# Where the weight split of the expert stages runs: ScalarE and VectorE in the place of GpSimd

## The reference

```
q = (ht @ w_q).reshape(T, 8, 2, 128)
s = einsum('thpd,hpkd->thpk', q, sub_keys)
top_s, top_i = top_k(s, 16)                     # per head and half: 16 of 128 keys
best_s, best_c = top_k(sums of the pairs, 16)   # 16 of 256 pairs -> 16 of 16384 experts
gates = softmax(best_s)
u = expert_u[expert_idx]; act = gelu(einsum('td,thkd->thk', x, u))
v = expert_v[expert_idx]; out = einsum('thk,thkd->td', gates * act, v)
```

## Time and profile before

| | |
|---|---|
| median of 3 runs | 4019.38 us (4003.71 to 4023.93) |
| profiled execution: span from the first to the last instruction | 3969.4 us |
| PE busy | 3562.3 us, 90% |
| DVE busy | 2298.1 us, 58% |
| POOL busy | 2306.4 us, 58% |
| ACT busy | 797.8 us, 20% |
| mean granted TensorE clock | 0.941 of 2.4 GHz |

### The profile page before, as it was taken

How to read it: one execution, slowest core, us unless ns; L and a number is a source line. 1 busy time by engine, 2 the same in 40 slices (tenths; PEclk the granted TensorE clock), 3 DMA queues, 4 the chain that set the end, 5 groups by cost and what they waited for, 6 DMA issues and landing times.

```text
span 3969.4 us, 47909 instructions
## 1 busy us (share of the span) xinstructions
PE 3562.3 (90%) x16820; PEld 2877.3 (72%) x16820; DVE 2298.1 (58%) x3373; ACT 797.8 (20%) x1199; POOL 2306.4 (58%) x1012
## 2 busy tenths in 40 slices
PE   8986997999988999989999998777777799999997
PEld 6554985787767787868768776666666688888885
DVE  2434443442177645452225998787777547887883
ACT  2223212111144311220121112222222111111110
POOL 5330003787745566648766886343434478888885
PEclk9997998999999999989999998888888899999998
DMA  3110001222211222212222343333333555555641
GB/s 129 48 38 1 1 1 43 80 95 90 96 64 66 66 74 78 70 58 96 85 90 101 127 135 116 113 117 112 129 120 114 193 200 200 183 179 189 214 138 69
DMA packets 146107, 408.58 MB, mean 103 GB/s; under 512 B 11192, under 2 KB 43960, under 8 KB 143680
## 3 DMA queue, kind: packets, MB, share of 16 engines
q1 hardware_dynamic: 73616, 266.37, 20.0%
q10 hardware_dynamic: 72368, 140.68, 10.1%
HBM read 337.80 MB, written 69.21 MB: 103 GB/s over the span
## 4 chain that ended last, share of the span: by engine, by line
PE 70%; DVE 19%; issue 7%; ACT 2%; DVEq 1%; ACTq 1%; DMA 0%; POOL 0%; POOLq 0%
PE bank L310 18%; PE bank L311 18%; PE bank L312 18%; DVE oneL L1665 2%; PE bank L333 1%; DVE oneH L1664 1%; ACT arena L851 1%; PE bank L805 1%; PE bank L807 1%; PE bank L503 1%; PE bank L517 1%; PE bank L745 1%; DVE arena L1640 1%; PE bank L507 1%; DVE arena L1566 1%
## 5 line engine op out<-in xcount | busy, mean ns | idle before, releaser
L1235 POOL TENSOR_TENSOR ring_hi<-ring,cst 128x1024 fp32r<-128x1024 f32 x504 | 1018.8, 2021 | 1591.0 <-PE bank L312 1576.0
L1237 POOL TENSOR_TENSOR ring_lo<-ring,ring_hi 128x1024 fp32r<-128x1024 f32 x504 | 1288.4, 2556 | 39.5
L310 PE MATMUL bank<-xs,ring_hi 128*128 128x512 f32 x2616 | 1076.2, 411 | 77.6 <-DVE xs L1256 50.8
L311 PE MATMUL bank<-xs,ring_hi 128*128 128x512 f32 x2616 | 1047.5, 400 | 0.0
L312 PE MATMUL bank<-xs,ring_lo 128*128 128x512 f32 x2616 | 1044.1, 399 | 0.0
L851 ACT ACTIVATE arena<-bank 128x512 f32<-128x512 f32 (+5 forms) x655 | 436.1, 684 | 1980.1 <-PE bank L312 1291.3
L310 PEld LDWEIGHTS bank<-xs,ring_hi 128*128 128x128 f32 x2616 | 511.3, 195 | 210.4 <-issue 66.0
L312 PEld LDWEIGHTS bank<-xs,ring_lo 128*128 128x128 f32 x2616 | 508.8, 194 | 112.4
L311 PEld LDWEIGHTS bank<-xs,ring_hi 128*128 128x128 f32 x2616 | 511.2, 195 | 102.8 <-issue 1.8
L310 PE MATMUL bank<-gw,ring_hi 128*128 128x512 f32 x1024 | 401.8, 392 | 0.8 <-ACT arena L851 0.7
L311 PE MATMUL bank<-gw,ring_hi 128*128 128x512 f32 x1024 | 398.8, 389 | 0.0
(11 more groups left out here) (255 smaller groups left out, 3725.5 us busy)
## 6 DMA issues: line engine op xcount, KB each, us to landing
ring<-weights SPq DMA_DIRECT2D x504, 512.0 KB, 3.3
hidden<-arena ACTq DMA_DIRECT2D x128, 256.0 KB, 2.2
gates<-arena ACTq DMA_DIRECT2D x16, 2048.0 KB, 7.6
arena<-hidden ACTq DMA_DIRECT2D x16, 2048.0 KB, 11.1
arena<-gates ACTq DMA_DIRECT2D x16, 2048.0 KB, 18.0
xres<-x_t ACTq DMA_DIRECT2D x4, 512.0 KB, 7.2
out_t<-arena SPq DMA_DIRECT2D x1, 2048.0 KB, 7.1
arena<-ret_decay ACTq DMA_DIRECT2D x1, 1024.0 KB, 5.6
```

Source lines behind the costliest of these rows:

```text
L310: pe.matmul(out_, wh, x[0], start=start, stop=False, skip_group_check=True)
L311: pe.matmul(out_, wh, x[1], start=False, stop=False, skip_group_check=True)
L1235: pool.tensor_tensor(ring_hi[:, r % 2, :], ring[:, r, :], one, ALU.mult).then_inc(split_hi, 1)
L1237: pool.tensor_tensor(ring_lo[:, r % 2, :], ring[:, r, :], ring_hi[:, r % 2, :].bitcast(F32), ALU.subtract).then_inc(w_split, 1)
```

## The change

From the gate stage on (block `B_S` = 295), POOL no longer splits. ACT makes the high part (`expert_hi`), DVE the low part (`expert_lo`), each for the block three ahead (`LEAD`) of the one whose product is just done. `ring_lo` is laid over `ring` (the split is in place), `ring_hi` has four buffers; so four blocks can stand split, and SP loads a slot again only when its block is used. In the value stage gated hidden, its parts and the sums are woven in block by block. POOL keeps the 295 blocks before, now limited by loads alone, and does blocks 295 to 297. PE's instructions and their order stay.

```
-        ring_hi = sb("ring_hi", [P, 2, D], F32R)
-        ring_lo = sb("ring_lo", [P, 2, D], F32R)
+        ring_lo = nc.alloc_sbuf_tensor_at("ring_lo", [P, RING, D], F32R, offset=nc.sbuf_base - RING * D * 4)
+        ring_hi = sb("ring_hi", [P, RING, D], F32R)
@@ SP
-                    sp.wait_ge(w_split, i * RING + (r + 1 - RING))
+                    sp.wait_ge(block_used, i * RING + (r + 1 - RING))
@@ PE
-                pe.wait_ge(w_split, it * per + (n + 1))
+                if n < B_S:
+                    pe.wait_ge(w_split, it * per + (n + 1))
+                else:
+                    pe.wait_ge(u_lo, it * per + (n - B_S + 1))
@@ ACT
+            def expert_hi(n, it=0, per=0):
+                r = n % RING
+                act.wait_ge(loaded[r], it * (4 * per) + 16 * (n // RING + 1))
+                A(ring_hi[:, r, :], ring[:, r, :], ACT.Copy).then_inc(u_hi, 1)
...
+            act.wait_ge(u_hi, LEAD)
             with act.Fori(0, NTG // 2) as i:
...
                         gelu(B_U + j0 + bb, q + bb, j0 + bb, i, 2 * NU_GATES)
+                        expert_hi(B_S + bb + LEAD, i, 2 * NU_GATES)
                         for u in (2 * b, 2 * b + 1):
...
+            def v_feed(g, it=0):
+                for b in range(JG):
+                    expert_hi(B_V + JG * g + b + LEAD, it, 2 * JG)
+                    gated_hi(g + 1, b, it)
+            v_feed(0)
             load(3)
             with act.Fori(0, NJG // 2 - 2) as i:
-                gated_hi(2, i)
+                v_feed(1, i)
                 load(4, i)
...
@@ POOL
-                if it is not None or r >= 2:
-                    pool.wait_ge(block_used, n - 1)
...
+            for n in range(B_S, B_S + LEAD):
+                split(n % RING, n - B_S, n // RING, u_hi, u_lo)
@@ DVE
+            def expert_lo(n, it=0, per=0):
+                r = n % RING
+                ve.wait_ge(u_hi, it * per + (n - B_S + 1))
+                TTN(ring_lo[:, r, :], ring[:, r, :], ring_hi[:, r, :].bitcast(F32), ALU.subtract).then_inc(u_lo, 1)
...
             with ve.Fori(0, NTG // 2) as i:
                 for u in range(2 * TG // 4):
+                    if u % 2 == 0:
+                        expert_lo(B_S + u // 2 + LEAD, i, 2 * NU_GATES)
                     ve.wait_ge(oh_pe, i * 16 + u + 1)
...
+            def v_feed(g, it=0):
+                for b in range(JG):
+                    expert_lo(B_V + JG * g + b + LEAD, it, 2 * JG)
+                    gated(g + 1, b, it)
+                    if b == 0 and g:
+                        acc(g - 1, 1, it)
+                    if b == 4:
+                        acc(g, 0, it)
+                    gated_lo(g + 1, b, it)
```

More of the change, by code:

```diff
@@ L68 @@
 N_LOADED = -(-N_BLOCKS // RING) * RING
+B_S = B_U + NU_ROUTE * TT
+LEAD = 3
 PARAMS = [("attn_pre", 8), ("attn_post", 8), ("mu", 15), ("w0", 4), ("a0", 4), ("k_k", 4), ("k_a", 4),
@@ L209, in build @@
         split_hi = sem("split_hi")
+        u_hi, u_lo = sem("expert_hi"), sem("expert_split")
         scaled = sem("scaled")
@@ L287, in _ @@
                 sp.dma_start(ring[:, r, :], wstream[r]).then_inc(loaded[r], 16)
-            with sp.Fori(1, N_LOADED // RING) as i:
+            with sp.Fori(1, N_BLOCKS // RING) as i:
                 for r in range(RING):
-                    sp.wait_ge(w_split, i * RING + (r + 1 - RING))
+                    sp.wait_ge(block_used, i * RING + (r + 1 - RING))
                     sp.dma_start(ring[:, r, :], wstream[bass.ds(i * RING + r, 1)].rearrange("a p n -> (a p) n")
                                  ).then_inc(loaded[r], 16)
+            for n in range(N_BLOCKS // RING * RING, N_BLOCKS):
+                sp.wait_ge(block_used, n + 1 - RING)
+                sp.dma_start(ring[:, n % RING, :], wstream[n]).then_inc(loaded[n % RING], 16)
             sp.wait_ge(out_ready, KD)
@@ L1189, in load, with gated_hi @@
                               ).then_inc(gld[b], 16)
[L1191 to L1194, removed]
+            def gated_hi(g, j, it=0):
+                act.wait_ge(ex_prod, it * 2 * JG + g * JG + j + 1)
+                A(GW[g % 2][j][0], tile(HV + 8 * (g % 2) + j), ACT.Copy).then_inc(ex_hi, 1)
             load(0)
             load(1)
+            n = B_U + j0 + LEAD
             with act.Fori(0, NU_REST // 4 - 1) as i:
@@ new lines, in acc @@
+            def acc(g, half, it=0):
+                ve.wait_ge(block_used, it * 2 * JG + B_V + g * JG + 4 * half + 4)
+                if g:
+                    ve.wait_ge(ex_acc, it * 16 + 8 * (g - 1) + 4 * half + 4)
+                for d in range(4):
+                    o = tile(ACC + 4 * half + d)
+                    TTN(o, o, bank[4 * half + d][:, :], ALU.add).then_inc(ex_acc, 1)
+            n = B_S + NU_GATES * NTG + LEAD
+            with ve.Fori(0, NU_REST // 4 - 1) as i:
+                for b in range(4):
+                    expert_lo(n + b, i, 4)
@@ new lines, in _ @@
+            n += NU_REST - 4
+            for b in range(4):
+                expert_lo(n + b)
+                gated(0, 2 * b)
+                gated(0, 2 * b + 1)
+                gated_lo(0, 2 * b)
+                gated_lo(0, 2 * b + 1)
+            def v_feed(g, it=0):
[7 more added lines that the diff above has]
+                    gated_lo(g + 1, b, it)
@@ L1710, in _ @@
+            v_feed(0)
+            with ve.Fori(0, NJG // 2 - 1) as i:
+                v_feed(1, i)
+                v_feed(2, i)
+            for b in range(JG - LEAD):
+                expert_lo(N_BLOCKS - JG + LEAD + b)
+                if b == 0:
+                    acc(NJG - 2, 1)
+            acc(NJG - 1, 0)
+            acc(NJG - 1, 1)
             ve.wait_ge(ex_acc, 8 * NJG)
```

83 lines of the change are left out of this document (33 added, 50 removed).

## The result

| | before | after |
|---|---|---|
| median time | 4013.93 us (4003.71 to 4023.93, 4 runs) | 4444.03 us (4419.32 to 4472.47, 4 runs) |
| ratio to before | 1 | 1.110, 95% interval 1.101 to 1.119 |
| span of the profiled run | 3969.4 us | 4419.2 us |
| gate stage, first to last unit | 705.1 us | 1136.3 us |
| its clock | 0.84 | 0.69 |

The change costs 11%. The spans differ by 449.8 us, the medians by 430.1. The profiled run of after lies at the lower end of its runs: 4420.95 us around a span of 4419.2. So the page's span and the time differ by under 2 us.

What follows compares the result with a forecast made beforehand. It took PE to bound the value stage, and PE and DVE to hold each other in the gate stage. Gate stage +414 and the passage after it +11 gave span 4394; 50 on top gave 4444 us, range 4300 to 4500.

Steps and rivals of the forecast that it cites:

- The chain: Gate stage: DVE's units queue behind a wait for the previous product, so nothing runs beside it; 17.57 us per block.
- Its terms: Gate stage, one block: gelu and store issue, high part, low part, two units, PE unit, product, hand-overs; 17.57 us.
- The clock rule: Gate stage: PE's restarts at the lower clock cost 1.97 us per block, 126 us over 64, against the skill's under 1%.
- Rival B: Gate stage: same chain, but clock stays at its upper level, 15.4 us per block, 4306 us; chance 7%.
- Gate to value stage: Last unit to last gelu: rest block 3's high part queues behind a store issue; +11 us, between 0 and +20.
- Value stage: Value stage: no change, as PE is the bound at 5.49 us per block; loss possible, gain not.
- Before the gate stage: Before 2427 us: no change, with splits falling elsewhere worth up to 14 us to either side.
- The sum: Whole kernel: +414 and +11 make +425 us, span 4394 us, median 4444 us.
- the 50 us put on top: Whole kernel: the median before lay 50 us above the profiled span, so the same was added to the predicted span.
- A: Gate stage: units do not wait for the product, 7.2 us per block, 3772 us; chance 5%.
- C: Gate stage: clock stays low through the product, 4738 us; chance 4%.
- D: Value stage: group loads hold ACT 14.0 us with high parts behind them, +27 us, 4471 us; chance 5%.

Runs made afterwards that it cites:

- e1: Changed kernel with DVE's low part placed between a gate block's two units, one block later; 3781.56 us, ratio to before 0.941.
- e6: Changed kernel with ACT making the high part twice per gate-stage block, same output; 4544.32 us.
- e8: Changed kernel with unused PE matmuls in each gate-stage block, 27 before the first unit and 6 before the second; 4314.25 us.
- e5: Changed kernel with POOL's old limit of two blocks put back for the 295 blocks before the gate stage; 4445.08 us.
- e2: Changed kernel with ACT's high part ahead of the gelu in the gate stage, DVE's order kept; 3962.05 us.
- e3: Changed kernel with 22 unused PE matmuls ahead of the units in each gate-stage block; 4415.94 us.
- e4: Changed kernel with POOL splitting the gate stage's blocks too, ACT and DVE beginning behind it; 3889.81 us, ratio to before 0.972.
- e7: e1 with POOL's splits of blocks 2 and 3 held back and the second group's loads issued 12 blocks later; 3774.81 us.
- e9: e4 with POOL's old limit of two blocks put back for all its 359 blocks; 4038.17 us.

## Why the prediction was right

**The chain, right and shown.** Units, high part, low part and product follow one another, since DVE's low part waits for ACT's high part, which waits for the product before. e1 changes the place of the low part and leaves the work, and the time falls by 675.8 us in the stage; e6 lengthens one link by 1.09 us and the period grows by that and 0.2 us of clock.

**Its terms.** For the period from 2728.30 to 2745.83, in the prediction's order: 1.21 (1.22), 1.09 with the hand-over (1.10), 1.14 (1.21), two units 5.45 with the hand-over (5.32), unit on PE 1.76 (1.77), product and hand-over 6.88 (6.56). The sum is 17.53; the prediction's values in brackets, with its 0.39 for hand-overs, give 17.57. But this is one of the short periods. The gelus around it start at 2691.49, 2710.28, 2728.30, 2745.83, 2763.19 and 2781.99, so periods of 18.79, 18.02, 17.53, 17.36 and 18.80, and the mean of the stage is 17.98. What varies is how much of the product runs at the lower level. In the period before this one three of the product's eight triples of matmuls have it, against two here:

```profile
2720.87 0.73 PE L319 MATMUL bank<-xs,ring_hi 128*128 128x512 f32 x1
...
2723.53 0.63 PE L319 MATMUL bank<-xs,ring_hi 128*128 128x512 f32 x1
...
2724.61 0.39 PE L319 MATMUL bank<-xs,ring_hi 128*128 128x512 f32 x1
```

So the term for the product was mis-sized: with its hand-over it is 7.37 in the mean, where the sum had 6.56 and 0.13. The trace of before already held this. Its 32 products behind an idle PE take 6.6 and 7.6 us in turn from the third on, 7.13 in the mean, and the earlier trace rows shows one of the short ones. This is the restart ahead of it, 7.59 us from the first line to the second:

```profile
2727.80 0.73 PE L310 MATMUL bank<-xs,ring_hi 128*128 128x512 f32 x1
...
2735.39 0.22 PE L805 MATMUL bank<-oneB,oneH 128*128 128x128 f32 x1
```

The product's term was 0.7 us too small and the others together 0.3 too large, which leaves 0.4 us per block, 26 us over the stage. Only 17 of them show in the difference, because the prediction set 64 whole periods against 710 us, while the marks in the table take in 63 and a step against 705.1.

**The clock rule.** The trace and e8 put the lower level at 2.4 us in each of 64 blocks (1.97 in the prediction, short by the product's term), 152 us, 3.4% of the span. The Trainium skill, "TensorE: Matmul & The Clock Gate", section "What's actually happening", holds the warm-up under 1% of a typical kernel's span. This kernel is not typical in that sense: it warms up 64 times. The rows decided rightly. Rival B, a clock at its upper level throughout, is refuted by the granted 0.50 of the units and the product's head.

**Gate to value stage.** +11 predicted, +9.6 measured. ACT, after:

```profile
3593.35 10.39 ACTq L1202 DMA_DIRECT2D arena<-hidden  x1
3603.78 3.51 ACTq L1204 DMA_DIRECT2D arena<-gates  x1
3607.55 0.60 ACT L860 ACTIVATE arena<-bank 128x512 f32<-128x512 f32 x1 [21.77 <-issue]
3608.32 8.06 ACTq L1148 DMA_DIRECT2D hidden<-arena  x1
3616.81 1.06 ACT L860 ACTIVATE ring_hi<-ring 128x1024 fp32r<-128x1024 f32 x1 [8.66 <-issue]
```

Step by step as forecast: two long issues, the gelu, a third long issue, and the high part behind it. PE starts block 3 at 35.2 us behind the last unit (37.6 in the sum) and needs 72.4 us from there to the last gelu (72.5).

**Value stage.** "Gain is not possible" was wrong, by 6.6 us. PE is busy 695.76 of 696 us where it was 702.87 of 703, for the same 24 matmuls in each of 128 blocks. A busy PE was taken for a PE at its fastest. In the timeline of before a matmul starts some 0.227 us after the last one, but from 3240 to 3920 us 45 starts are later, by 5.6 us together, as here at the change from one block to the next:

```profile
3333.49 0.39 PE L312 MATMUL bank<-gw,ring_lo 128*128 128x512 f32 x1
3333.89 0.49 PE L310 MATMUL bank<-gw,ring_hi 128*128 128x512 f32 x1
3334.22 0.39 PE L311 MATMUL bank<-gw,ring_hi 128*128 128x512 f32 x1
```

The two steps are 0.40 and 0.33 us; records of 0.39 us that overlap hide them from a view of busy time. From 3700 to 4380 us of after no start is late. That is 5.6 of the 6.6 us; what delayed them before was not tested. Another 1.0 us lies behind the stage, in the closing norm.

**Before the gate stage.** 0 predicted with ±14, +16.5 measured. 9.5 of it is in place by the first exponential of attention. The start on DVE, after:

```profile
23.66 3.06 DVE L1310 SCALAR_TENSOR_TENSOR arena<-xres,par,arena 128x512 f32<-128x512 f32 x2
26.63 2.83 DVE L1285 TENSOR_TENSOR xs<-arena,xs 128x512 fp32r<-128x512 f32 x1
...
35.22 0.68 DVE L1285 TENSOR_TENSOR xs<-arena,xs 128x512 fp32r<-128x512 f32 x1
```

and before:

```profile
24.26 1.41 DVE L1281 SCALAR_TENSOR_TENSOR arena<-xres,par,arena 128x512 f32<-128x512 f32 x2
25.78 0.69 DVE L1256 TENSOR_TENSOR xs<-arena,xs 128x512 fp32r<-128x512 f32 x1
```

POOL now splits blocks 2 and 3 from 23.82 to 33.96 us, where it had stopped after two, and DVE's instructions take up to four times as long beside it. The prediction had named this collision, for the route stage, and missed it at the start. e5 takes the collision away and still ends attention no earlier, since the clock is lower there. Nor is 16.5 a firm number: in e1, e2, e3, e4, e6 and e8, whose program is that of after up to the gate stage, the first unit comes at 2434.5 to 2444.6 us once the excess of the long form (last section) over the 283.0 of after is taken off, so the profile of after is the latest of seven that spread by 13 us. The miss is then rather 3 to 17 us against the one profile of before, and its cause stays open.

**The sum.** Spans: +425 predicted, +449.8 measured, off by 24.8: +17 in the gate stage, +16.5 before it, -1.4 between, -7.6 behind, apart from rounding. The median was met to 0.03 us by luck: the 50 us put on top, which were no overhead, covered 25 us that the sum lacked, and the runs fell into two groups. 4013.93 + 449.8 would be 4464, and the four runs lie at 4419 to 4421 and 4467 to 4472, with the median between the two.

Of the rivals, A (faster, 3772 us) was wrong for this order, and its price right: it is what e1 reaches, 3781.56. C's clock would have been near 0.5 in the stage and was 0.69. D did not come: the value stage grew shorter.

## What to carry to other kernels

An instruction that works ahead must not stand, on an engine that takes its list in order, in front of work that another engine wants now. Place it where everything it waits for is long done: the stage took 1136 us with the low part in one place and 460 us with it in another. When splitting work off a shared engine, list for each moved instruction every waiting instruction ahead of it (e2 failed on this), and look also at what the lifted limits let the old engine do: here that half of the change was worth -102 us. Before a sum is trusted, read each term in several periods in a row, since one may be an extreme of a pattern, as the product of 6.56 us was in a series of 6.6 and 7.6.

## What the runs showed of the hardware

**A busy PE at the lower level.** Between attention and the trunk there is a stretch of small matmuls, from some 335 us on, the same in every kernel here. It takes 283 to 284 us in before, after and e4, and 325 to 333 us in e1, e2, e3, e6, e7, e8 and e9 (308 in e5). Busy by stretch of the same 50 us, in after and in e1:

```profile
550.00:600.00 50.00, 49.22 (x594) 40.54 (x593) 19.90 (x41) 1.79 (x3) 0.00 (x0) 1.00 0.01 2
```

```profile
550.00:600.00 50.00, 49.22 (x397) 42.91 (x396) 17.78 (x36) 0.00 (x0) 0.00 (x0) 0.50 0.00 1
```

PE is busy 49.22 of 50 us in both, yet the granted clock is 1.00 in one and 0.50 in the other, with two thirds of the matmuls done. It is the likely cause of the 45 us between runs of one kernel: the seven runs of before beside e1 have one span of 3969.1 us, with a mean clock of 0.941, and six of 4015.0 to 4024.4, with 0.926 to 0.928. What decides which of the two a run gets stays open. It is also the reason why the 50 us above the span in the prediction were no overhead.

**Short gaps and the clock.** In e3, with two gaps of 1.23 and 1.54 us left in a block of 17.2 us, the second unit and the head of the product ran at the lower level; with both filled, e8 kept 1.00 throughout.

**POOL beside DVE.** A subtraction of two 128x512 tiles on DVE (L1285) took 0.68 us alone and 2.83 us beside POOL's splits. The Trainium skill, "SBUF — State Buffer", section "Who interferes with whom", names the ports that the two share, and the trace agrees. e4 against e9 adds that the same splits cost 1.7 us per block more or less, by whether POOL must wait for PE before it makes them.
